# Rotation and doubling of q and k by partition copies issued from GpSimd, in place of matmuls with 0/1 matrices

## What is computed

```python
def apply_rope(t, positions):                     # first block only: q (16 heads) and k (4 heads)
    half = HEAD_DIM // 2                          # HEAD_DIM = 64
    inv_freq = ROPE_THETA ** (-jnp.arange(half, dtype=jnp.float32) * 2.0 / HEAD_DIM)
    ang = positions.astype(jnp.float32)[..., None] * inv_freq
    cos, sin = jnp.cos(ang)[:, :, None, :], jnp.sin(ang)[:, :, None, :]
    t1, t2 = t[..., :half], t[..., half:]
    return jnp.concatenate([t1 * cos - t2 * sin, t2 * cos + t1 * sin], axis=-1)
...
        q = apply_rope(q.astype(f32).reshape(b, s, ATTN_HEADS, HEAD_DIM), positions)
        k = apply_rope(k.astype(f32).reshape(b, s, KV_HEADS, HEAD_DIM), positions)
        attn = sliding_window_sink_attention(q, k, v, sinks[i]).astype(x.dtype)
...
    s_sel = jnp.einsum('bhqgd,bhqkld->bhqgkl', qs, kg)    # second block: k of two branches, no rotation
    s_win = jnp.einsum('bhqgd,bshd->bhqgs', qs, kw)
```

## Time and profile before

| | |
|---|---|
| three runs | 2822.74, 2822.82, 2825.5 us |
| median | 2822.82 us |
| span of the profiled execution | 2820.8 us, 2.0 under the median |
| TensorE busy | 2776.5 us, 98% |
| VectorE, ScalarE busy | 1944.5 us (69%), 1388.5 us (49%) |
| GpSimd busy | 43.8 us |
| mean granted TensorE clock | 0.995 of full speed |

### The profile page before, as it was taken

How to read it: one execution, slowest core, us unless ns; L and a number is a source line. 1 busy time by engine, 2 the same in 40 slices (tenths; PEclk the granted TensorE clock), 3 DMA queues, 4 the chain that set the end, 5 groups by cost and what they waited for, 6 DMA issues and landing times.

```text
span 2820.8 us, 41566 instructions
## 1 busy us (share of the span) xinstructions
PE 2776.5 (98%) x16736; PEld 2430.6 (86%) x16736; DVE 1944.5 (69%) x2802; ACT 1388.5 (49%) x2076; POOL 43.8 (2%) x82
## 2 busy tenths in 40 slices
PE   8999999999999999999999999998999999999998
PEld 7888888888888888888888889987888888888887
DVE  7448677757766665566656779877788775578764
ACT  6335555544454443344454551347555553455543
POOL 0310000000000000000000000000000000000000
PEclk9999999999999999999999999998999999999999
DMA  7447445565656556655656556533455546555554
GB/s 238 152 141 222 146 153 157 172 193 188 194 179 193 191 180 195 193 184 187 196 174 206 184 165 209 155 120 117 133 170 197 192 176 203 189 179 191 198 190 139
DMA packets 147728, 503.51 MB, mean 178 GB/s; under 512 B 17296, under 2 KB 24192, under 8 KB 147280
## 3 DMA queue, kind: packets, MB, share of 16 engines
q1 hardware_dynamic: 142000, 489.35, 53.6%
q0 software_dynamic: 3664, 7.29, 0.9%
q10 hardware_dynamic: 1872, 4.20, 0.4%
HBM read 496.55 MB, written 7.41 MB: 179 GB/s over the span
## 4 chain that ended last, share of the span: by engine, by line
PE 92%; DVE 4%; ACT 2%; issue 1%; DMA 0%; ACTq 0%; SPq 0%; DVEq 0%
PE PS L833 91%; ACT wh L1297 1%; DVE CC L1864 1%; DMA raw<-in_w_in 0%; PE PS L1214 0%; DVE TA L1856 0%; DVE TC L1864 0%; ACT TB L1297 0%; DVE Z L1856 0%; DVE BIGt L1864 0%; ACT BIGt L1297 0%; DVE wl L1856 0%; DVE H L1856 0%; DVE H L1864 0%; DVE RB L1907 0%
## 5 line engine op out<-in xcount | busy, mean ns | idle before, releaser
L1856 DVE TENSOR_TENSOR wl<-raw,wh 128x1024 fp32r<-128x1024 f32 (+1 forms) x888 | 1038.4, 1195 | 503.0 <-ACT wh L1297 501.1
L1297 ACT ACTIVATE wh<-raw 128x1024 fp32r<-128x1024 f32 (+1 forms) x888 | 893.5, 1031 | 551.9 <-PE PS L833 481.5
L833 PE MATMUL PS<-CHt,wh 128*128 128x512 f32 x2816 | 885.9, 395 | 1.5 <-DVE wl L1856 1.5
L833 PE MATMUL PS<-BIGt,wh 128*128 128x512 f32 (+1 forms) x2432 | 684.1, 367 | 2.4 <-issue 0.9
L833 PEld LDWEIGHTS PS<-CHt,wl 128*128 128x128 f32 x2816 | 529.0, 188 | 124.7
L833 PE MATMUL PS<-AHt,wh 128*128 128x512 f32 (+1 forms) x1984 | 604.8, 385 | 14.4 <-DVE wl L1856 11.4
L833 PE MATMUL PS<-CHt,wl 128*128 128x256 f32 x2816 | 553.6, 278 | 0.0
L833 PEld LDWEIGHTS PS<-BIGt,wl 128*128 128x128 f32 x2112 | 398.0, 188 | 78.8
L833 PE MATMUL PS<-BIGt,wl 128*128 128x256 f32 x2112 | 443.4, 279 | 0.0
L833 PEld LDWEIGHTS PS<-CHt,wh 128*128 128x128 f32 x2816 | 429.4, 189 | 1.9 <-issue 1.8
L833 PEld LDWEIGHTS PS<-AHt,wl 128*128 128x128 f32 x1856 | 350.9, 189 | 75.3
(11 more groups left out here) (303 smaller groups left out, 1632.1 us busy)
## 6 DMA issues: line engine op xcount, KB each, us to landing
raw<-in_w_up SPq DMA_DIRECT2D x264, 512.0 KB, 4.5
raw<-in_w_in SPq DMA_DIRECT2D x232, 512.0 KB, 3.7
raw<-in_w_down SPq DMA_DIRECT2D x132, 512.0 KB, 4.0
raw<-in_w_gate SPq DMA_DIRECT2D x88, 512.0 KB, 4.4
raw<-in_w_down SPq DMA_DIRECT2D x56, 384.0 KB, 3.3
raw<-in_w_ssd_br SPq DMA_DIRECT2D x32, 512.0 KB, 4.3
raw<-in_w_o SPq DMA_DIRECT2D x32, 512.0 KB, 4.3
raw<-in_w_ple_gate SPq DMA_DIRECT2D x32, 512.0 KB, 4.0
```

The source lines that it names most:

```text
L833: return e.matmul(o, l, r, start=start, stop=stop, skip_group_check=True)
L1297: return e.activation(o, x, f, **k)
L1856: return e.tensor_tensor(o, x, y, op)
```

## The change

The four rotations of q, the rotation and doubling of k, and the two doublings in the second block become transfers between partitions, issued by GpSimd. `turn_heads` copies each run of 32 partitions of a tile to the neighbouring run (four copies of 64 KB: 32 partitions of 2 KB); the sign goes into the table SIN, through the sign of the frequencies. `twice` copies each half of k to both halves (four copies of 128 KB: 64 partitions of two rows of 1 KB). k is now rotated first, in place, by three operations of VectorE, and doubled afterwards. q has two buffers (RQ), so that each set of copies may run beside the rotation before. The 0/1 matrices are gone from the constants (320 KB less to load). The plan gets empty steps between the phases: one more after each `rope_q`, and the stages of `rope_k` are of one phase and of two with a delay of one and an empty step.

```diff
-            gens=([stage("rotary", 0, 3)] if i == 0 else []) + [stage("rope_q", i, 2)])
-    add("w_in", ..., "ev_k", 0, mode="turn", gens2=[stage("full_u1", 0, 4)], gens=[stage("rope_k", 0, 2), stage("rope_k", 1, 2)])
+            gens=([stage("rotary", 0, 3)] if i == 0 else []) + [stage("rope_q", i, 2, 0, (0,))])
+    add("w_in", ..., "ev_k", 0, mode="turn", gens2=[stage("full_u1", 0, 4)], gens=[stage("rope_k", 0, 1), stage("rope_k", 1, 2, 1, (0,))])
...
 pool_program
+        def turn_heads(dst, src, sem):
+            for r in range(4):
+                e.dma_start(dst[32 * r:32 * r + 32], src[32 * (r ^ 1):32 * (r ^ 1) + 32]).then_inc(sem, 16)
+
+        def twice(dst, sem):
+            for hp in range(2):
+                for half in range(2):
+                    e.dma_start(dst[64 * half:64 * half + 64].rearrange("p (t h) n -> p t h n", h=2)[:, :, hp, :],
+                                (KT1 if sem is kdu_in else KTC)[64 * hp:64 * hp + 64, :, :]).then_inc(sem, 16)
+
+        def rope_q(i, ph):
+            if ph:
+                return
+            e.wait_ge(evq_d.sem, evq_d.at(i))
+            if i >= 2:
+                e.wait_ge(rq_d.sem, rq_d.at(i - 2, "q"))
+            else:
+                e.wait_ge(rot_a.sem, rot_a.at(0, "aex"))
+            turn_heads(RQ[i % 2], QT[:, 2 * i:2 * i + 2, :], rq_in[i % 2])
+
+        def rope_k(t, ph):
+            if t == 0 and ph == 0:
+                e.wait_ge(evk_d.sem, evk_d.at(0))
+                e.wait_ge(rq_d.sem, rq_d.at(2, "q"))
+                turn_heads(RQ[0], KT1[:, :, :], rk_in)
+            elif t == 1 and ph == 1:
+                e.wait_ge(rk_d.sem, rk_d.at(0, "k"))
+                twice(KDU[:, :, :], kdu_in)
+
+        def dup_k2(br, ph):
+            if ph == 0:
+                e.wait_ge(k2_d.sem, k2_d.at(br))
+                if br == 0:
+                    e.wait_ge(jn_d.sem, jn_d.at(0, "ms"))
+                twice(KD2[:, br, :, :], kd2_in[br])
...
 tensor_program (its rope_q, rope_k and dup_k2 are removed)
         def attn1(t, ph):
...
-                e.wait_ge(rk_d.sem, rk_d.at(j // 2, "kd"))
+                e.wait_ge(kdu_in, 4 * 16)
...
 attn2, phase "sc0"
-                e.wait_ge(dk_d.sem, dk_d.at(1, "t1"))
+                if t == 0:
+                    for br in range(2):
+                        e.wait_ge(kd2_in[br], 4 * 16)
...
 vector_program
         def rope_q(i, ph):
...
-                tt(x, bank(6), two(SIN[:, :]), MUL).then_inc(rq_d.sem)
+                e.wait_ge(rq_in[i % 2], 64 * (i // 2 + 1))
+                tt(x, x, two(SIN[:, :]), MUL).then_inc(rq_d.sem)
...
         def rope_k(t, ph):
...
+            o, x = KT1[:, :, :], RQ[0]
+            if t == 1 and ph == 0:
+                e.wait_ge(rk_in, 64)
+                tt(x, x, two(SIN[:, :]), MUL).then_inc(rk_d.sem)
+                tt(o, o, two(COS[:, :]), MUL).then_inc(rk_d.sem)
+                e.wait_ge(rk_d.sem, rk_d.at(0, "y"))
+                tt(o, o, x, ADD).then_inc(rk_d.sem)
...
         def ev_k2(n, u):
             if u.i:
-                e.wait_ge(dk_pe.sem, 1)
+                e.wait_ge(kd2_in[0], 4 * 16)
```

More of the change, by code:

```diff
@@ L55 @@
 MIXER = 'a0 g0 m0 a1f m1f g1 a2 k0S k1fS g2 v0h v1 q0S2 a3fh g3 q1 q2fh q3fh xCh yS'.split()
-MATS = ["rot", "rdup0", "rdup1", "triu", "negT", "dup0", "dup1", "ident", "ones"]
+MATS = ["triu", "negT", "ident", "ones"]
 VECS = [("g_mix", 16), ("cw", 96), ("cb", 24), ("g_ssd", 16), ("dsk", 16), ("g_ffn", 16), ("g_ple", 16),
@@ L183, in all_units @@
             banks=(3, 4) if i == 1 else (0, 1, 2),
[L184 to L185 removed]
+            gens=([stage("rotary", 0, 3)] if i == 0 else []) + [stage("rope_q", i, 2, 0, (0,))])
+    add("w_in", 0, 16, 1024, "U1", "ev_k", 0, mode="turn", gens2=[stage("full_u1", 0, 4)], gens=[stage("rope_k", 0, 1), stage("rope_k", 1, 2, 1, (0,))])
     add("w_in", 0, 16, 1280, "U1", "ev_v", 0, nc=288, more=6656, nat=True, mode="nat",
@@ L673, in hybrid_block_kernel @@
     k2_d, v2_a = steps("ev_k2"), steps("ev_v2", "c0", "c1")
-    dk_pe, dk_d = steps("dup_k2_pe"), steps("dup_k2_d", "t0", "t1")
+    kd2_in = [dma("k2_twice0"), dma("k2_twice1")]
     q2_d = steps("ev_q2")
@@ L973, in norm @@
             tok.then_inc(nrm_pe.sem)
[L975 to L995, removed]
         def attn1(t, ph):
@@ L1148, in compress @@
                 tok.then_inc(cp_pe.sem)
[L1150 to L1162, removed]
         def after_odd(p):
@@ L1974, in rope_k @@
         def rope_k(t, ph):
[L1975 to L1984, removed]
-                tt(KDU[:, 2 * t:2 * t + 2, :], x, y, ADD).then_inc(rk_d.sem)
+            o, x = KT1[:, :, :], RQ[0]
[5 more added lines that the diff above has]
+                tt(o, o, x, ADD).then_inc(rk_d.sem)
         def attn1(t, ph):
@@ L2383, in ev_k2 @@
             tt(KTC[:, :, :], bank(u.bank), two(RU[:, 0:T]), MUL).then_inc(k2_d.sem)
-        def dup_k2(br, ph):
-            if ph:
-                e.wait_ge(dk_pe.sem, br + 1)
-                for t in range(2):
-                    e.tensor_copy(KD2[:, br, 2 * t:2 * t + 2, :], bank(5 + t)).then_inc(dk_d.sem)
         def ev_q2(n, u):
@@ L2664, in _constants @@
     eye = np.eye(P, dtype=np.float32)
-    rot = np.zeros((P, P), np.float32)
-    for m in range(P):
-        if m % 64 < 32:
-            rot[m + 32, m] = -1.0
-        else:
-            rot[m - 32, m] = 1.0
-    dup = []
-    for hp in range(2):
-        e = np.zeros((P, P), np.float32)
-        e[hp * 64 + i % 64, i] = 1.0
-        dup.append(e)
-    rdup = [(rot[:, hp * 64 + i % 64]).copy() for hp in range(2)]
     triu = (i[:, None] <= i[None, :]).astype(np.float32)
     negt = np.where(i[:, None] <= i[None, :], 0.0, NEG).astype(np.float32)
-    mats = [rot, rdup[0], rdup[1], triu, negt, dup[0], dup[1], eye, np.ones((P, P), np.float32)]
+    mats = [triu, negt, eye, np.ones((P, P), np.float32)]
     mats = np.ascontiguousarray(np.concatenate(mats, 1))
```

35 lines of the change are left out of this document (15 added, 20 removed).

## The result

The changed kernel takes **2868.1 us** (median of four runs, 2866.9 to 2870.4) against 2823.5 for the kernel before on the same chip: a ratio of 1.0157, 95% interval 1.0144 to 1.0170. It is slower by 44.6 us. The forecast was 2854.3, +31.5, with a range up to 2867: direction and main mechanism were right, the size was 13 us short and the time lies 1 us outside the range. The profiled execution has a span of 2865.1, 44.3 above the 2820.8 of before.

The account below looks back on a forecast made before the run. TensorE, busy 98% of the span, was taken to bound the kernel. Lateness 33.0, slow clock 2.1 and attention 1 1.0, less 4.6 in the second attention, gave +31.5 on 2822.8: 2854.3 us, 8-in-10 range 2846 to 2867.

Parts of the forecast that it names:

- Steps 1 and 2: Before attention 1: the v projection ends at 84.0, and the q copies are hidden, costing VectorE 0.
- Step 3: GpSimd's lookup ahead of the k copies: ends at 143.6, bounds 140.8 and 147.2, taking 3.3 us a cycle.
- Step 4: k turned, rotated and doubled behind the lookup: scores may start at 155.2, bounds 153.5 and 158.
- Steps 5 and 6: TensorE reaches attention 1's scores at 115.4, waits 39.8 us, and is 33.0 us late against before.
- Step 7: VectorE's backlog behind the wait, ahead of TensorE's transposes: the cover just holds, 0, up to 2 us if not.
- Step 8: TensorE's restart at half clock after the long wait: 2.1 us lost, bounds 0 and 2.9.
- Step 9: Attention 1 five H groups later, more of it among split weights: +1.0 us, bounds -1 and +5.
- Step 10: Second attention: both doublings go, -4.6 us, with the copies covered by over 40 us.
- the stall spreads: Rival after the stall: VectorE carries its backlog on, TensorE waits again for masks and splits; 2865 and above; 12 in 100.
- main case: TensorE's stall before attention 1's scores lasts 36 to 44 us, time 2848 to 2865; 75 in 100.
- faster: Rival on GpSimd's queue: it matters less, half the lookup's copies issue faster than shown; 2811 to 2822; 2 in 100.

Follow-up runs that it names:

- the run with q alone: Kernel before with only q turned by copies, k and the second attention left on matmuls: 2820.8 us, ratio 0.9990.
- the run with the lookup moved: Changed kernel with GpSimd's whole lookup placed behind the four copies that double k: 2825.5 us, ratio 1.0009.
- the relieved kernel: Kernel before with the 31-tap convolution's last two units cut to 64 of 256 columns and second-attention k doubled by copies: 2818.7 us; control without copies 2824.3.
- the kernel of before with the place alone: Kernel before, all matmuls kept and no copies, attention 1's scores behind nine H groups instead of four: 2835.5 us, ratio 1.0041.
- the run with the later load: Changed kernel with GpSimd issuing the second load of the input one evacuation later: 2867.7 us, ratio 1.0155.
- the version that beats both: All rotations and doublings by copies, lookup behind the copies of k, attention 1 at its old place: 2815.4 us, ratio 0.9970 against the kernel before.
- the one with the second attention alone: Kernel before with only the doubling of k in the second attention done by copies: 2822.9 us against 2824.2, ratio 0.9995.

## Why the prediction was right, and where it fell short

**Steps 1 and 2** held. The v projection ended at 83.6 (84.0 forecast), and the copies of q cost nothing, which the run with q alone shows by itself.

**Step 3**, the end of the lookup: 146.0 against 143.6. The first large copies came as assumed (the fourth at 119.78, 119.2 forecast); the four cycles from there took 15.05, not 13.2, with 3.65 to 3.83 a cycle where I had taken 3.3. The end lies inside the bounds. The 4.2 of before was no firm figure for full queues: its four cycles took 3.6 to 4.7, while the DMA engines were busy 51 to 79%, so there was less to win from quiet ones.

The Trainium skill (DMA: Bandwidth & Descriptors, "Anatomy of one DMA") has 2.0 us plus the bytes at 436 KB per us. With the issue of 0.56 this makes an estimate of 3.5 for 384 KB; the trace had 3.65 to 3.83 beside quiet queues, so nearer to it than to my 3.3, and a little over it.

**Step 4**, from the lookup's end to the scores: 10.35 against 11.6. The turned k landed after 1.9 us (2.7 taken), the doubled after 2.7 (3.0 taken).

**Steps 5 and 6**: the wait was 41.5 (39.8), the lateness 34.1 (33.0). That this wait would come, where, what would end it and how long it would last was right, and the run with the lookup moved shows that its cause was too.

**Step 7**, VectorE's backlog, held: 0. **Step 8**, the slow restart, was 2.6 against 2.1: a wait of 41.5 us ended at 0.50, and the clock rose only between 160 and 164.

**Step 9** is the term that failed: 9.1 us where +1.0 stood, with a bound of +5. New waits of over 5 us between 170 and 300 were the sign that the prediction had named for it; they came to 8.3. The cause was named rightly, more of attention 1 among split weights. It was sized by VectorE's mean, 31.3 busy of 40, as if idle time could be spent anywhere. A softmax goes back and forth between VectorE and ScalarE, and at each handover it stands behind splits, which themselves wait for loads. A mean load of 78% does not show that. The bound should have come from the wait of this kind in the other attention, 5.38 for PT2a, and the slow clock behind it, which I had counted after the long stall alone; two of these make 2 x (5.38 + 2.1) = 15 us.

**Step 10** failed too: -4.6 was forecast, -1.5 came. The 2.85 and 1.72 were right (the relieved kernel gives 4.5 of 4.57), and so was the cover for the copies. What I did not ask was who is next: VectorE is busy 20.00 of 20 us at 1800 to 1820 in the kernel before, shown below, while TensorE is at 20.00 as well. A matmul taken from the one leaves the other.

```profile
1800.00:1820.00 20.00, 20.00 (x153) 20.00 (x153) 20.00 (x43) 8.78 (x14) 0.00 (x0) 1.00 0.51 156
```

The misses add up: 1.1 + 0.5 + 8.1 + 3.1 = 12.8 of the 44.3 - 31.5. **The rival "the stall spreads"** gave 2865 and above and so had the time, but not for its reason: it let VectorE carry a backlog out of the stall, and the kernel of before with the place alone has the same two waits without any stall. Its 12 in 100 should have been a part of the main case. **The break-even** of the rival "faster" (k doubled by 115.4) was met in the runs with the lookup moved: k is there before TensorE wants it, and what then decides the sign is the place of attention 1.

**What the place costs**, counted from the first scores with nine groups done: 10.8 us in the kernel of before with the place alone, 10.8 in the changed one with the lookup moved, 9.1 in the changed one. The waits differ little (7.6, 7.2 and 7.0 over the 1.33). The rest is the clock behind the second wait: it falls to 0.50 in the first two (243 to 245 and 237.5 to 239.5 in their traces), which costs 1.7 us in each, and stays at 1.00 in the changed kernel (279 to 283). So it is the clock and not the stall ahead that makes the difference: the run with the later load has the same stall, and its clock fell there too.

**Open**: why the clock falls behind the second wait in some of these executions and not in others. And that the softmax is late because of the splits was read from the time lines of one head and from the place; no run took splits away from beside it.

## What to carry to other kernels

An engine that only issues transfers is a queue too: before moving work onto it, write down everything that stands ahead, issues and waits for landings both, and compare with the time at which the consumer wants the result. Where the order is free, put the short copies that someone waits for ahead of the long ones that no one waits for; here that one move decided 42 of 45 us. And a step taken off the busiest engine is worth its length only where the next engine has room in that very stretch, read as a window and not as a mean over the span.

## What the chip showed that I had not expected

**A fall of the clock behind a wait of 1.74 us, in some executions only.** At one place, some 206 us behind the marker, TensorE waits 1.74 us for Z. In the kernel before (at 491.04) the clock stays at 1.00. In the kernel with q alone it falls behind the same wait; its time line and, under it, the stretch that follows:

```profile
487.85 0.50 PE L848 MATMUL PS<-AHt,wh 128*128 128x512 f32 x1 [1.74 <-DVE Z L1862]
```

```profile
488.00:492.00 4.00, 4.00 (x16) 3.47 (x17) 1.65 (x2) 0.63 (x1) 0.00 (x0) 0.62 0.54 158
```

It costs 1.6 us (from the marker to the first matmul of BLK and W1V are 1445.0 us with it and 1443.4 without), and four of the twelve profiled executions have it (q alone, the place alone, the version that beats both, and the later load). A second such place lies in the second attention. From its first scores to the end it is 990.8 us in the profiled executions of the kernels before and after the change, and 991.1 to 993.0 in the ten others; between 90 and 100 us behind these scores the granted clock is 0.98 in the kernel before, where it is 0.89 in the one with the second attention alone (992.4). A third is the wait for SX1b in attention 1, above. So spans of single executions compare no better than to 2 or 3 us here, and a marker ahead of such places is the better measure for what lies before it.

**Copies between partitions of the same memory** land after 1.9 us (64 KB, quiet queues, median), 2.7 (128 KB, quiet), 4.2 (64 KB, beside the weight loads of 40 to 70) and 4.8 (128 KB, beside those of the second attention). Their issue by GpSimd takes 0.50 to 0.60 each, so a set of four is issued in 2.0 to 2.4.
